# A three-block fp32 transformer kernel on one core: the first pair of each MLP reordered, one more tile with seven products, decay tables made later

## The reference

```python
def _mlp(x, norm_g, w1, w2):                 # w1: 1024 x 4096, w2: 4096 x 1024
    h = _rmsnorm(x, norm_g)
    return jnp.square(jax.nn.relu(h @ w1)) @ w2

def _retention_dir(q, k, v, log_gamma, strict):
    lg = log_gamma[:, None]                  # log_sigmoid of the learned decays, 8 heads
    diff = pos[:, None] - pos[None, :]
    dmask = jnp.where(allowed[None], jnp.exp(lg[:, :, None] * jnp.maximum(diff, 0.0)[None]), 0.0)
    ...
    a = jnp.einsum('bhid,bhjd->bhij', qc, kc) * dmask

for layer in range(2):
    x = x + (_even_mixer if layer == 0 else _odd_mixer)(...)
    x = x + _mlp(x, mlp_norm[layer], w_mlp_in[layer], w_mlp_out[layer])
```

## Time and profile before

| | |
|---|---|
| median of 3 runs | 981.22 us (981.2 to 981.59) |
| profiled execution, its own time | 979.64 us |
| its span, first to last instruction | 977.8 us, mean granted clock 0.995 |
| PE busy | 961.5 us (98% of the span), 5810 matmuls |
| DVE busy | 766.8 us (78%) |
| ACT busy | 606.7 us (62%) |
| POOL busy | 130.0 us (13%) |
| DMA | 174.80 MB, mean 179 GB/s |

### The profile page before, as it was taken

The page is one execution under the profiler, slowest core; times in us unless marked ns, Lnnn a source line. Parts: engine busy times, 40 slices in busy tenths (PEclk is TensorE's granted clock), DMA queues, the critical chain, the costliest instruction groups (busy, mean ns, idle before and its releaser), DMA issues.

```text
span 977.8 us, 15188 instructions
## 1 busy us (share of the span) xinstructions
PE 961.5 (98%) x5810; PEld 847.1 (87%) x5810; DVE 766.8 (78%) x1157; ACT 606.7 (62%) x1003; POOL 130.0 (13%) x173
## 2 busy tenths in 40 slices
PE   9999989999999999999998999999999999999997
PEld 8878879999998888888887999999888888988885
DVE  6888687999975767786657889885758989878884
ACT  6688665777765554455455766664535867766662
POOL 2731023022001102220002000000550110000000
PEclk9999999999999999999999999999999999999999
DMA  9984544647572663345455456564444463633631
GB/s 338 307 225 184 174 155 147 226 134 244 187 244 87 215 214 131 129 133 212 173 172 172 173 189 234 180 234 166 151 155 168 138 207 99 204 130 129 215 129 44
DMA packets 110342, 174.80 MB, mean 179 GB/s; under 512 B 4288, under 2 KB 73024, under 8 KB 110272
## 3 DMA queue, kind: packets, MB, share of 16 engines
q1 hardware_dynamic: 109840, 173.40, 52.6%
q10 hardware_dynamic: 432, 0.44, 0.1%
HBM read 172.78 MB, written 1.05 MB: 178 GB/s over the span
## 4 chain that ended last, share of the span: by engine, by line
PE 92%; DVE 5%; issue 1%; ACT 1%; POOL 0%; POOLq 0%; DVEq 0%
PE ps L472 19%; PE ps L473 19%; PE ps L474 19%; PE ps L579 11%; PE ps L532 8%; PE ps L530 5%; DVE wlo L1648 2%; PE ps L548 2%; PE ps L743 1%; PE ps L723 1%; PE ps L529 1%; PE ps L546 1%; PE ps L711 1%; PE ps L667 1%; DVE arena L1775 1%
## 5 line engine op out<-in xcount | busy, mean ns | idle before, releaser
L1648 DVE TENSOR_TENSOR wlo<-raw,whi 128x1024 fp32r<-128x1024 f32 (+1 forms) x312 | 364.3, 1196 | 26.9 <-ACT whi L1111 26.6
L1111 ACT ACTIVATE whi<-raw 128x1024 fp32r<-128x1024 f32 (+1 forms) x312 | 310.0, 1024 | 47.4 <-PE ps L474 30.2
L472 PE MATMUL ps<-hT,whi 128*128 128x256 f32 x584 | 165.9, 284 | 0.0
L474 PE MATMUL ps<-hT,wlo 128*128 128x256 f32 x584 | 165.4, 283 | 0.0
L473 PE MATMUL ps<-hT,whi 128*128 128x256 f32 x584 | 165.4, 283 | 0.0
L472 PE MATMUL ps<-whi,hT 128*128 128x512 f32 (+1 forms) x312 | 122.1, 391 | 0.0
L474 PE MATMUL ps<-whi,hT 128*128 128x512 f32 (+1 forms) x312 | 120.1, 385 | 0.0
L473 PE MATMUL ps<-wlo,hT 128*128 128x512 f32 (+1 forms) x312 | 120.0, 385 | 0.0
L532 PE MATMUL ps<-hT,whi 128*128 128x512 f32 x336 | 119.7, 396 | 0.0
L472 PEld LDWEIGHTS ps<-hT,whi 128*128 128x128 f32 x584 | 111.7, 191 | 1.7 <-issue 0.3
L473 PEld LDWEIGHTS ps<-hT,whi 128*128 128x128 f32 x584 | 111.7, 191 | 1.3
(11 more groups left out here) (253 smaller groups left out, 1632.8 us busy)
## 6 DMA issues: line engine op xcount, KB each, us to landing
raw<-in_w SPq DMA_DIRECT2D x64, 1024.0 KB, 5.4
raw<-in_w_in SPq DMA_DIRECT2D x34, 1024.0 KB, 4.9
raw<-in_w_in_o SPq DMA_DIRECT2D x24, 1024.0 KB, 5.1
raw<-in_w_out_o SPq DMA_DIRECT2D x8, 1024.0 KB, 4.9
raw<-in_w_in_e SPq DMA_DIRECT2D x5, 1024.0 KB, 13.0
raw<-in_w_mem SPq DMA_DIRECT2D x4, 1024.0 KB, 10.1
raw<-in_w_out_e SPq DMA_DIRECT2D x4, 1024.0 KB, 4.8
raw<-in_w_out SPq DMA_DIRECT2D x4, 1024.0 KB, 4.9
```

The costliest lines, as they stand in the source:

```text
L472: e.matmul(o, a[0], b[0], start=start, stop=False)
L474: return e.matmul(o, a[1], b[0], start=False, stop=stop)
L1111: e.activation(split_half(i)[0], raw_half(i), ACT.Copy).then_inc(*up("hi", ("hi", i)))
L1648: e.tensor_tensor(l, raw_half(i), h.bitcast(F32), ALU.subtract).then_inc(*up("lo", ("lo", i)))
```

## The change

Three edits. Pair 0 of each MLP makes its u before further weight halves. Tile 12 joins `SEVEN`, and `PLAIN` moves from 12 to 13. In the first MLP the tables for the decays are scaled at j = 14 and 15 (four heads each) instead of j = 5 to 8 (two each), the exponentials move from j = 12 to 15 into the `rq` tiles c = 3 to 6, and POOL's series waits for u of pair 11. The values' first copy on ACT gets a wait for the last added table.

```diff
--- before.py
+++ after.py
@@ -51,8 +51,8 @@
 XK, XV = 17408, 18432
 EO, ED, EB = 16656, 16784, 17040
 SP = 257
-SEVEN = (1, 2, 3, 5, 6, 7, 9, 10, 11)
-PLAIN = 12
+SEVEN = (1, 2, 3, 5, 6, 7, 9, 10, 11, 12)
+PLAIN = 13
 WIDE_UP = ((0, 1), (1, 0), (1, 1), (2, 0))
 WIDE = ((1, 0), (1, 1), (2, 0), (2, 1))
 
@@ -1359,9 +1359,9 @@
                 for j in range(17):
                     i = second(layer, j)
                     if j < 16:
-                        weights_to(i + 6)
+                        weights_to(i + (6 if j else 4))
                         relu_squared(layer, j)
-                        weights_to(i + 7)
+                        weights_to(i + (7 if j else 5))
                         u_high(layer, j)
                     else:
                         used(("w2", layer, 15), 1)
@@ -1393,12 +1393,8 @@
                 e.activation(us[j % 2][0][:, k0:k1, :], SQ2[j % 2][:, k0:k1, :], ACT.Copy).then_inc(*up("xh", ("uh", layer, j)))
 
             def decays(j):
-                if 12 <= j < 16:
-                    dd = dtab[:, 2 * (j - 12):2 * (j - 12) + 2, :]
-                    w.wait_ge(*at("dtab", j - 12))
-                    e.activation(dd, dd, ACT.Exp).then_inc(*up("ex", ("dec", j - 12)))
-                if 5 <= j < 9:
-                    for h in (2 * j - 10, 2 * j - 9):
+                if 14 <= j < 16:
+                    for h in range(4 * j - 56, 4 * j - 52):
                         w.wait_ge(*at("dlo"))
                         e.activation(dtab[:, h, :], cst[:, C_U:C_U + 384], ACT.Copy, scale=lgt[:, 96 + h:97 + h])
                         e.activation(dtmp[:, h, :], cst[:, C_L:C_L + 384], ACT.Copy, scale=lgt[:, 104 + h:105 + h]).then_inc(
@@ -1420,8 +1416,16 @@
                     w.wait_ge(*at("t", ("rq", c), m))
                     e.activation(qk_high[c // 4][h], (oqT if c < 4 else okT)[:, h, :], ACT.Copy).then_inc(*up("xh", ("th", c, m)))
 
+            def decay_exp(c):
+
+                dd = dtab[:, 2 * c:2 * c + 2, :]
+                w.wait_ge(*at("dtab", c))
+                e.activation(dd, dd, ACT.Exp).then_inc(*up("ex", ("dec", c)))
+
             for c in range(8):
                 used(("rq", c), 1)
+                if 3 <= c < 7:
+                    decay_exp(c - 3)
                 for m in range(2):
                     low_copied(("rq", c), m, (oqT if c < 4 else okT)[:, 2 * (c % 4) + m, :])
                 if c:
@@ -1443,6 +1447,7 @@
                 for tb in range(2):
                     w.wait_ge(*at("mm", ("rv", c), tb))
                     w.wait_ge(*at("rs", "ret", tb))
+                    w.wait_ge(*at("dtab", 3))
                     if c >= 2:
                         w.wait_ge(*at("rv", 2 * c - 3))
                     e.activation(VH[c % 2][:, tb, :], bank("mm", ("rv", c), tb), ACT.Copy, scale=stats(("r", "ret", tb), 1)).then_inc(
@@ -2084,10 +2089,10 @@
                 for j in range(17):
                     i = second(layer, j)
                     if j < 16:
-                        weights_to(i + 5)
+                        weights_to(i + (5 if j else 3))
                         if j < PLAIN:
                             u_sums(layer, j)
-                        weights_to(i + 7)
+                        weights_to(i + (7 if j else 4))
                         u_low(layer, j)
                     else:
                         used(("w2", layer, 15), 1)
@@ -2463,6 +2468,7 @@
                 w.wait_ge(*at("dexp"))
                 e.tensor_scalar(t1, e_, 2.0, None, ALU.add).then_inc(*up("po", ("dp2",)))
                 w.wait_ge(*at("drec"))
+                w.wait_ge(*at("ul", 0, 11))
                 chained(e.tensor_tensor(s_, e_, t1, ALU.mult), 0)
                 chained(e.tensor_tensor(s2, s_, s_, ALU.mult), 1)
                 chained(e.tensor_scalar(pl, s2, 1.0 / 19, 1.0 / 17, ALU.mult, ALU.add), 2)
```

## The result

The changed kernel takes 967.62 us (median of 4 runs, 967.4 to 967.91), the kernel before 981.21 us beside it (979.67 to 981.59). The ratio is 0.9865, with a 95% interval of 0.9848 to 0.9882. The forecast was 968.2 us, with a range of 966.8 to 971.8.

What follows compares the result with a forecast made beforehand. PE was taken as the bound (busy 931 of 940 us), with time to win in its two waits for u, by fewer matmuls or at the ends. -12.0 - 1.4 + 0.4 = -13.0 from 981.2 gave 968.2 us, range 966.8 to 971.8.

Steps and rivals of the forecast that it cites:

- The first u: Pair 0 of each MLP: u made earlier removes PE's wait and the slow matmuls behind it, 6.0 us each, -12.0 us.
- The rolled chain: ACT and DVE steps to the first u, at old durations: `u_low` at 139.8, 1.07 us before PE asks.
- The slow matmuls: Start of each MLP, behind PE's wait: eight matmuls at the 1.2 GHz level, 1.7 us of the 6.0.
- the three terms: The summands of the forecast: first u -12.0 us, tenth tile -1.4, decay tables +0.4.
- No debt at pairs 1 to 3: DVE work passed over in pair 0 delays nothing: margins 2.2 us, then about 1 us; price on the path 0.
- the prediction's rival: Pairs 1 to 3: DVE or a weight load 2 us later makes PE wait, 970.2 to 972.2 us; chance 0.12.
- The tenth tile: Tile 12 in `SEVEN`: 3 matmuls fewer in each layer, -1.4 us; DVE's added 3.5 us a layer covered by slack.
- The tables: End of first MLP: POOL's table additions meet three `sums_shared` operations on DVE, +0.4 us, ends 0 and 1.4.
- No other cost: Exponentials in the `rq` stretch, the values' new wait, `row_scales` and ACT's weight copies at pair 14: each 0.
- The rival "slower": Seven-product pairs: DVE as bound, each short wait brings eight matmuls at 1.2 GHz, up to 1012 us; chance 0.02.

Runs made afterwards that it cites:

- e1: Kernel before with only pair 0 of each MLP making its u before further weight halves: 968.34 us, ratio 0.9878.
- e6b: Changed kernel with ACT's old order in pair 0 put back and DVE's new order kept: 970.07 us, ratio 0.9897.
- e2: Kernel before with only tile 12 added to `SEVEN` and `PLAIN` at 13: 978.87 us, ratio 0.9988.
- e5: Kernel before with only the decay tables' edit (scaled at pairs 14 and 15): 980.47 us, ratio 1.0001.
- e3: Changed kernel with the decay tables left where they were before (scaled at pairs 5 to 8): 967.0 us, ratio 0.9865.
- e4: Changed kernel with the tables scaled at pairs 13 and 14 and POOL's series released by u of pair 10: 967.1 us, ratio 0.9864.
- e7: Changed kernel with tile 8 added to `SEVEN` too: 966.71 us, ratio 0.9863.
- e8: Changed kernel with tiles 4 and 8 added to `SEVEN` too: 968.11 us, ratio 0.9876.
- e6: Changed kernel with DVE's old order in pair 0 put back and ACT's new order kept: 984.81 us, ratio 1.0049.
- e9: Changed kernel with tile 13 added to `SEVEN` and `PLAIN` at 14: 970.53 us, ratio 0.9901.

## Why the prediction was right, step by step

- **The first u.** Forecast -12.0 us, measured -11.89 (6.04 and 5.85, e1 against before). The rolled chain held to a tenth: the high part of u was done at 139.1, where 138.8 was rolled in a trace that runs 0.32 us earlier, and `u_low` at 140.09 against 139.8; the margin is 1.10 against 1.07. e6b shows that the margin hangs on both engines.
- **The slow matmuls** were part of this sum: 1.7 us in each MLP. In the profile of before there were 8 and 7 (1.69 and 1.55 us above the full pace); e2 and e5 have 8 to 14, and 14 of them cost 2.95 us. So the 1.7 was right for the execution that it was read from and low for others. This bears on the medians: they differ by 981.21 - 967.62 = 13.6 us, the two profiled executions by 979.64 - 967.4 = 12.2. The prediction carried the 1.6 us between profile and median of before over to the changed kernel, whose profiled execution stands only 0.2 below its median. So the sum of -13.0 is 0.8 too large between the profiled executions and 0.6 too small between the medians, and that the absolute forecast came out within 0.6 us is in part luck: the 981.2 rested on three runs, and in the later rounds the median of before was 980.2 to 980.4 over 7 or 15 runs, 12.6 to 12.8 above the changed kernel. Of the 0.8, 0.32 is the longer stage ahead, which the edits don't touch, and 0.38 the three terms, which measure 12.62 us in the two MLPs. That the slow stretch makes the spread of before is not shown run by run; the granted clocks of e2's runs fit it.
- **No debt at pairs 1 to 3.** Right: margins of 2.6 and 1.1 us in place of the 2.2 and about 1 that were worked out, and no such wait in the changed kernel, e1, e3, e4 or e7. The debt is real all the same: in e6b, with u some 1 us later, PE loses 0.32 us behind pair 2, as the prediction's rival had it.
- **The tenth tile.** -1.4 us, measured -1.36 (e1 to e3), with DVE's added work in slack: over 265 to 303 us DVE is busy 27.1 us before and 31.4 in the changed kernel. Right.
- **The tables.** +0.4, measured 0.62 (e3 and e4 against the changed kernel). This is the term of the sum that was mis-sized. I took the middle between no meeting and three; the trace shows all three, at 0.76 us each. The prediction's own figure for three, a delay of 0.6 us, is what came. The Trainium skill's rule (SBUF — State Buffer, "Who interferes with whom") called for this: a VectorE operation with two SBUF inputs contends with a GpSimd instruction that reads SBUF, and the one issued first blocks the other. The trace agrees: each of the three sums began beside an addition with about 0.95 us still to run, and took 0.76 us more. It agrees also where nothing was lost: `u_low` of pair 15, at 295.11, began 0.44 us ahead of the first addition and took 0.69 us, and the first addition to x, with an operand in PSUM, took 0.75 us wholly beside the fourth.
- **No other cost.** The exponentials, the new wait of the values, `row_scales` and ACT's copies at pair 14 were taken at 0: from the fourth group of L667 to the sixth it is 198.12 us in the changed kernel and 198.13 before, and in the first MLP the three terms alone give what was measured, -6.04 - 0.68 + 0.62 = -6.10. Right.
- **The rival "slower"** had short waits bring back 1.2 GHz. The runs speak against its premise: after waits of 0.46 and 0.7 us the matmuls went on 0.23 us apart. And in e8, where DVE is the bound, the pauses of about 0.1 us left the granted clock at 1.00.

## What to carry to other kernels

Where an engine makes both weights and the one thing that the bound engine waits for, put that one thing first at a stage's start and roll every engine of the chain: moving only one (e6) made it worse. Read what a moved step meets on the engines' shared memory, and whether that stands right ahead of the path: the same three meetings cost nothing in e5 and 0.6 us in the changed kernel. Find the pairs in which the second engine recovers before removing them: tile 8 was free, tile 4 cost more than it gave.

## What the runs showed of the hardware

- How long TensorE stays at 1.2 GHz after a wait of about 4.1 us differs between executions: 8 and 7 matmuls of 512 columns in the profile of before, 14 and 12 in e2, 13 and 8 in e5. When it falls differs too. PE in order of time in e5_tables, behind the first wait and behind the second:

```profile
145.42 0.79 PE L472 MATMUL ps<-whi,ur 128*128 128x512 f32 x1 [4.15 <-DVE ur L2057]
...
150.70 0.63 PE L472 MATMUL ps<-whi,ur 128*128 128x512 f32 x1
151.13 0.44 PE L473 MATMUL ps<-wlo,ur 128*128 128x512 f32 x1
...
525.72 0.50 PE L472 MATMUL ps<-whi,ur 128*128 128x512 f32 x1 [4.10 <-DVE ur L2057]
...
526.52 0.48 PE L472 MATMUL ps<-whi,ur 128*128 128x512 f32 x1
...
528.08 0.63 PE L473 MATMUL ps<-wlo,ur 128*128 128x512 f32 x1
```

  Behind the first, the matmuls start some 0.43 us apart at once. Behind the second, three start at the full pace (525.72 to 526.52) and the next eight are slow: the clock fell only when PE was at work again.
- The spread of the runs is wider in the kernels with the two waits: 1.8 to 2.2 us over 15 runs of before, 2.8 and 1.8 over eleven of e2 and e5, 2.2 over four of e6. It is 0.5 to 1.2 us over four runs in each kernel without the long waits. Fewer runs also show less spread, so part of this may be their number.
- A wait of 0.46 or 0.7 us left the pace at 0.23 us a matmul; 2.5 us was followed by slow transposes and four slow matmuls (e9), 4.1 by 7 to 14, 6.1 by 13 (e6, in both MLPs).
- Small GpSimd operations on 16 columns took 0.22 us or up to 1.10 us, by where they fell beside DVE. POOL and DVE in order of time in the changed kernel:

```profile
262.37 0.22 POOL L2476 TENSOR_TENSOR lgt<-lgt 128x16 f32<-128x16 f32 x1
262.68 1.10 POOL L2477 TENSOR_SCALAR lgt<-lgt 128x16 f32<-128x16 f32 x1
...
262.42 2.38 DVE L1653 TENSOR_TENSOR wlo<-raw,whi 128x1024 fp32r<-128x1024 f32 x2
```

  The first began just before a low half on DVE (two SBUF inputs), the second inside it, and it ended 0.11 us after that half did (263.67). In the kernel before, while DVE was idle from 155.96 to 159.68, such operations took 0.22 to 0.25 us each.
